# Attention scores on all 128 rows of the PE array: a full-height staging pair with placing DMAs, three weight buffers, keys' tiles ahead of queries' tiles

## The chip, the core and the metric

The kernel runs on one core of one Trainium2 chip. Inputs are in HBM; the working set lives in SBUF (128 partitions), matrix products go to eight PSUM banks of 128 x 512 fp32. The metric is the device time of one launch in microseconds (us), the median of the runs shown; one execution is taken with the hardware profiler and gives the rows below.

## What is computed

A decoder trunk of two layers on 512 tokens of width 1024. Each layer normalises x, projects it (one wide input projection), runs three token mixers in parallel, gates and merges them, and adds a gated per-layer embedding:

```python
h = rmsnorm(x, norm_g[i]);  proj = h @ w_in[i]
# A: 8 heads x 64, causal, with a cumulative log-forget bias
s = q @ k.T * 64**-0.5 + c[q] - c[k];  ya = softmax(s) @ v * silu(za)
# B: 8 query heads in 2 KV groups x 64: compressed, selected and sliding-window branches
yb = (g0*o_cmp + g1*o_sel + g2*o_win) * silu(zb)       # q and k rotated (rope)
# C: 4 heads, two 64-wide softmax maps each, 128-wide values
w = softmax(q1 @ k1.T) - lam * softmax(q2 @ k2.T);  yc = rmsnorm(w @ v) * silu(zc)
merged = sigmoid(mg_a)*(ya @ w_br_a) + sigmoid(mg_b)*(yb @ w_br_b) + sigmoid(mg_c)*(yc @ w_br_c)
x = x + merged @ w_out;  x = x + sigmoid(x @ w_ple_gate) * (p @ w_ple)
```

Every head's q and k are 64 wide. So a score product contracts over 64 rows, half of the PE array's 128.

## The kernel before

**Number format.** Each fp32 operand is split into a high part (rounded to the fp32r format) and a low part (the rest), and a product is three passes: hi x hi, lo x hi, hi x lo. `dense` does this for a weight tile: lines L731, L732, L733, each a matmul of 128 x 128 weights with 128 x 512 columns.

**Dense tiles.** A layer's weights come as 128-column tiles: `qa0` to `qa3` (queries of branch A, two heads each), `ka`, `va`, `za` (gate), then the same for B and C (`qb`, `ksb`, `kwb`, `vsb`, `vwb`, `zb`, `qc`, `kc`, `vc`, `zc`), the mixing gates `mga`/`mgb`/`mgc`, the branch projections `bra`/`brb`/`brc`, and `w1k`/`w1v`, four tiles each of a small hidden layer that compresses keys and values. A tile of `w_in` is 8 steps of three matmuls; `bra`, `brb`, `brc` have 4 steps; a `w1k` or `w1v` tile has 4 steps of two 256-column matmuls and is thus much shorter on PE than the others, though its weights are as large. SP loads a tile into one of RAW = 4 slots of `raw` (L589), ACT rounds it to `w_hi` in two halves (L1044), DVE subtracts to `w_lo` in two halves (L1278). `w_hi` and `w_lo` have two slots, so the conversion of tile t+2 starts when tile t is done. Results alternate between PSUM banks D0 and D1: tile t+2 may start only once ACT and DVE have emptied tile t's bank.

**Queries and keys.** For `qa` and `ka`, ACT copies the bank to a high part (L1111) and DVE makes the low part (L1425), straight into the places from which the scores read them. Rotated tiles (`qb`, `ksb`, `kwb`, `qc`, `kc`) are copied by ACT (L1120), SP swaps quarters of 32 partitions with four DMAs (L630), POOL multiplies by the sine (L683), DVE adds (L1519), ACT and DVE write high and low parts (L1151, L1521). A place holds two heads (or the two KV groups, or the two maps of C), one on partitions 0 to 63 and one on 64 to 127.

**Scores.** An attention unit is two heads; there are 12 units a layer, 0 to 3 of A, 4 to 7 of B, 8 to 11 of C. For a block i of 128 queries, an `S` step computes the scores of both heads against (i + 1) x 128 keys: three passes, in each one matmul on array rows 0 to 63 and one on rows 64 to 127 (L878), plus for A one more such pair that adds the forget bias (L884). The halves write to different banks, S0 and S1. A and C have one S step per block, B two (`sel`, `win`): 64 a layer, 128 in all. DVE masks and takes the maximum (L1530), ACT takes the exponential (L1158), PE transposes (L897, "T"), DVE or ACT copies (L539, L537), PE multiplies with the values (L919, "V").

**Order.** `make_schedule` writes one list of items, and every engine walks it. A stage s holds the attention steps of unit s and the dense tiles of `dense_tiles()[s]`; stage -1 comes ahead of all attention. Attention steps are spread among the dense steps; what follows a tile (swap, rot, ht, vcmp) comes a fixed number of dense steps after its end. Each engine is strictly in order, SP's queue too: a wait in front of one DMA holds up all DMAs behind it.

**After the attention** come a loop of `mgc` and `brc` tiles, `out`, and `gate`/`ple` tiles; ACT, DVE and PE walk the first two with hardware loops (`Fori`).

## Time and profile before

| | |
|---|---|
| median of 3 runs | 1543.6 us (1542.96 to 1544.0) |
| the profiled execution | 1546.29 us, of which the span from first to last instruction is 1544.5 us |
| mean granted clock of PE | 0.993 of full |
| PE busy (matmul) | 1500.4 us, 97% |
| PE weight loads, beside it | 1207.1 us, 78% |
| DVE / ACT / POOL busy | 942.2 (61%) / 636.7 (41%) / 75.3 us (5%) |
| all DMA queues | 129.49 MB, 31% of the 16 engines |
| dense matmuls, of the busy time | L731, L732, L733: 67% of the chain that ended last |
| score matmuls | L878: 768, L884: 64 |

A line of the profile is one group of instructions: line of the kernel, engine, operation, output<-inputs, shape, count. A matmul's shown duration includes the latency of the array, and matmuls overlap; what one costs is read from the distance between starts. A row of the timeline joins instructions of the same line that follow each other (xN). PEld is the weight load, which normally runs while the matmul ahead is still going. SPq is the queue of SP, which issues the DMAs.

### The profile page before, as it was taken

To read this page: it belongs to the slowest core of one execution; us is meant where nothing else is said; L and a number is where in the kernel's file an instruction comes from. 1 tells how busy PE (TensorE), PEld (TensorE's weight loads), DVE (VectorE), ACT (ScalarE), POOL (GpSimd) and SP (SyncE) were. 2 spreads that over 40 slices of the span, in tenths; PEclk is the share of its full clock that TensorE was granted. 3 is DMA by queue.
4 is the path that set the end of the run, shared out by engine and by line. 5 is a ranking of instruction groups with operands and counts; after the bars stand their busy time and mean duration, and the time that the engine had idled before them with its cause. 6 is when DMAs were issued, how large, how long until landed. Compare 5 with 4: busy or idle time off the path is not lost.

```text
span 1544.5 us, 22618 instructions
## 1 busy us (share of the span) xinstructions
PE 1500.4 (97%) x7957; PEld 1207.1 (78%) x7957; DVE 942.2 (61%) x2197; ACT 636.7 (41%) x1499; POOL 75.3 (5%) x80
## 2 busy tenths in 40 slices
PE   8999999999999999999999999999999999999997
PEld 6777777887787777888787787787887787788885
DVE  6866755555657776454576667655555676754544
ACT  6533434433344443343444334334333444334343
POOL 1000000000000010000100000000000000000011
PEclk9999999999999999999999999999999999999998
DMA  7223332222223332332342324222222233233321
GB/s 196 83 83 89 96 75 60 58 69 62 69 62 96 93 79 83 95 109 72 106 108 69 103 80 115 59 54 63 63 62 76 73 92 89 69 96 102 89 85 73
DMA packets 250300, 129.49 MB, mean 84 GB/s; under 512 B 45690, under 2 KB 245972, under 8 KB 250196
## 3 DMA queue, kind: packets, MB, share of 16 engines
q1 hardware_dynamic: 250196, 128.13, 31.1%
q8 instruction: 61, 1.00, 0.3%
q14 instruction: 43, 0.35, 0.1%
HBM read 118.67 MB, written 2.10 MB: 78 GB/s over the span
## 4 chain that ended last, share of the span: by engine, by line
PE 86%; DVE 6%; ACT 4%; issue 2%; DMA 1%; SPq 0%; POOL 0%; ACTq 0%; POOLq 0%; DVEq 0%
PE D L731 24%; PE D L733 22%; PE D L732 21%; PE Ob L919 7%; PE S L878 5%; PE T L897 4%; DVE w_lo L1278 2%; ACT w_hi L1044 1%; ACT probs L1158 1%; PE Mb L935 1%; PE Mb L845 1%; PE Ob L923 1%; PE Mb L812 1%; DVE probs L1530 0%; DVE y_lo L1612 0%
## 5 line engine op out<-in xcount | busy, mean ns | idle before, releaser
L731 PE MATMUL D<-h_hi,w_hi 128*128 128x512 f32 x1264 | 543.6, 430 | 12.5 <-DVE zs L1429 4.3
L733 PE MATMUL D<-h_lo,w_hi 128*128 128x512 f32 x1264 | 496.9, 393 | 0.0
L732 PE MATMUL D<-h_hi,w_lo 128*128 128x512 f32 x1264 | 495.2, 392 | 0.0
L1278 DVE TENSOR_TENSOR w_lo<-raw,w_hi 128x512 fp32r<-128x512 f32 (+2 forms) x504 | 295.2, 627 | 310.2 <-ACT w_hi L1044 310.1
L1044 ACT ACTIVATE w_hi<-raw 128x512 fp32r<-128x512 f32 (+2 forms) x504 | 264.7, 572 | 316.1 <-PE D L733 314.7
L731 PEld LDWEIGHTS D<-h_hi,w_hi 128*128 128x128 f32 x1264 | 239.2, 189 | 72.6 <-issue 20.8
L1158 ACT ACTIVATE probs<-probs,nmax 128x128 f32<-128x128 f32 (+3 forms) x256 | 141.9, 555 | 355.8 <-DVE nmax L1530 355.8
L733 PEld LDWEIGHTS D<-h_lo,w_hi 128*128 128x128 f32 x1264 | 237.9, 188 | 53.2
L732 PEld LDWEIGHTS D<-h_hi,w_lo 128*128 128x128 f32 x1264 | 240.1, 190 | 30.8 <-issue 0.5
L1530 DVE CUSTOM_DVE_ANT_0 probs<-S,maskb 128x128 f32<-128x128 f32 (+3 forms) x256 | 115.2, 487 | 49.2 <-PE S L878 30.3
L539 DVE COPY pT<-T 128x128 f32<-128x128 f32 (+3 forms) x160 | 77.6, 487 | 53.1 <-PE T L897 52.6
L919 PEld LDWEIGHTS Ob<-v_b,pT 128*128 128x128 f32 x640 | 90.5, 191 | 12.4 <-ACT pT L537 2.0
L897 PE MATMUL T<-ident,probs 128*128 128x128 f32 x560 | 98.0, 273 | 2.0 <-ACT probs L1158 2.0
L878 PE MATMUL S<-arena 64*128 64x384 f32 (+3 forms) x768 | 93.7, 349 | 0.9 <-DVE arena L1425 0.9
L731 PE MATMUL D<-y_hi,w_hi 128*128 128x512 f32 x224 | 93.9, 419 | 0.4 <-DVE y_lo L1612 0.4
L897 PEld LDWEIGHTS T<-ident,probs 128*128 128x128 f32 x560 | 72.3, 140 | 28.0 <-ACT probs L1158 5.6
L878 PEld LDWEIGHTS S<-arena 64*128 64x128 f32 x768 | 57.0, 185 | 45.5 <-issue 41.6
L733 PE MATMUL D<-y_lo,w_hi 128*128 128x512 f32 x224 | 87.9, 392 | 0.0
L732 PE MATMUL D<-y_hi,w_lo 128*128 128x512 f32 x224 | 87.5, 391 | 0.0
L919 PE MATMUL Ob<-v_b,pT 128*128 128x64 f32 x640 | 85.5, 264 | 0.3
L683 POOL TENSOR_TENSOR rb<-rs,sinT 128x512 f32<-128x512 f32 x28 | 36.4, 1300 | 970.0 <-DMA rs<-rx 596.0
L919 PEld LDWEIGHTS Ob<-v_ac,pT 128*128 128x128 f32 x480 | 67.7, 193 | 14.6 <-DVE pT L539 7.3
(243 smaller groups left out, 1499.3 us busy)
## 6 DMA issues: line engine op xcount, KB each, us to landing
raw<-in_w_in_dram SPq DMA_DIRECT2D x124, 512.0 KB, 3.9
raw<-in_w_in_dram SPq DMA_DIRECT2D x32, 256.0 KB, 3.7
raw<-in_w_out_dram SPq DMA_DIRECT2D x16, 512.0 KB, 4.0
raw<-in_w_ple_gate_dram SPq DMA_DIRECT2D x16, 512.0 KB, 4.1
rs<-rx SPq DMA_DIRECT2D x80, 64.0 KB, 2.0
raw<-in_cmp_w_k_dram SPq DMA_DIRECT2D x8, 512.0 KB, 3.8
raw<-in_cmp_w_v_dram SPq DMA_DIRECT2D x8, 512.0 KB, 3.8
raw<-in_w_br_a_dram SPq DMA_DIRECT2D x16, 256.0 KB, 2.9
```

Source lines behind the costliest of these rows:

```text
L539: eng.tensor_copy(pT[:, k % 2, 0:n], Tr[k % 2][:, 0:n]).then_inc(M["pt_dve_s"], 1)
L683: pool.tensor_tensor(rb[:], rs[:], sinT[:], ALU.mult).then_inc(M["pool_rot"], 1)
L731: pe.matmul(o, w_hi[:, sl, cs], hi[:, k, :], start=(k == 0), stop=False)
L732: pe.matmul(o, w_lo[:, sl, cs], hi[:, k, :], start=False, stop=False)
L733: ins = pe.matmul(o, w_hi[:, sl, cs], lo[:, k, :], start=False, stop=last)
L878: ins = pe.matmul(Sc[h][:, 0:n], qx[ps, qs], kx[ps, 0:n], start=(step == 0), stop=last)
L897: ins = pe.transpose(Tr[k % 2][:, j * P:(j + 1) * P], src[:, j * P:(j + 1) * P], ident[:])
L919: ins = pe.matmul(Ob[:, oc], pT[:, k % 2, j * P:(j + 1) * P], vs(j), start=(j == 0), stop=(j == i))
L1044: A(w_hi[:, sl, half], raw[:, ring(L, t, RAW), half], ACT.Copy).then_inc(M["act_hi"], 1)
L1158: A(probs[:, r % NP_, 0:n], probs[:, r % NP_, 0:n], ACT.Exp, scale=-1.0, bias=nmax[:, r % 8:r % 8 + 1], accum_out=sums[:, u % 2, i, c:c + ...
L1278: TT(w_lo[:, sl, half], raw[:, ring(L, t, RAW), half], f(w_hi[:, sl, half]), ALU.subtract).then_inc(M["dve_lo"], 1)
L1530: dve.tensor_tensor_reduce(probs[:, r % NP_, 0:n], Sc[r % 2][:, 0:n], maskb[:, S - n:S], -1.0, 3.0e38, ALU.add, ALU.min, nmax[:, r % 8:r % ...
```

## The change

1. **Scores on the whole array.** A query place now holds, for each head, high part and low part above each other on the 128 partitions; a key place holds for each head the high part twice and the low part twice. One matmul with the high keys then gives hi x hi and lo x hi at once, a second one with the low keys hi x lo and lo x lo. An S step becomes two matmuls per head on all 128 rows (L898, L899), with a third per head for A's bias (L902): four instead of six, or six instead of eight, and head 0 is complete before head 1 starts.
2. **Staging and placing.** ACT and DVE write the parts into one pair of buffers, `new_hi` and `new_lo`, and SP moves them to their places with four DMAs per tile (L659): of 64 x 512 for a query tile (512 KB in all), of 64 x 1024 for a key tile (1 MB in all). The S step that opens a unit waits for these DMAs (semaphore `put_s`); the next tile's write of `new_hi` waits for the placing of the one before.
3. **Room for it:** RAW is 3 instead of 4; `rb` is gone, the sine product is made in `rs` itself, so a swap now waits for DVE's use of the last one; `vbd` has its own buffer.
4. **Order of tiles:** in stage -1 `ka0` comes ahead of `qa0`; stages 1 to 3 are arranged anew; after `w1v3` the transposes `ht` and `vcmp` come 12 and 16 steps later instead of 6 and 8.
5. The hardware loops of ACT and DVE after the attention are written out (PE's stay), and a copy of the bias rows (L1473) is gone.

```diff
-RAW = 4
+RAW = 3
...
-    st = {-1: [("va", 0), ("va", 1), ("va", 2), ("va", 3), ("fg", 0), ("qa", 0), ("ka", 0), ("qa", 1)]}
+    st = {-1: [("va", 0), ("va", 1), ("va", 2), ("va", 3), ("fg", 0), ("ka", 0), ("qa", 0), ("qa", 1)]}
     st[0] = [("kcb", 0), ("ka", 1), ("za", 0), ("w1k", 0)]
-    st[1] = [("qa", 2), ("ka", 2), ("w1k", 1), ("ksb", 0), ("w1k", 2), ("za", 1)]
-    st[2] = [("qa", 3), ("w1k", 3), ("ka", 3), ("za", 2), ("vcb", 0)]
-    st[3] = [("qb", 0), ("w1v", 0), ("kwb", 0), ("w1v", 1), ("za", 3), ("w1v", 2), ("vsb", 0), ("w1v", 3), ("vwb", 0)]
+    st[1] = [("qa", 2), ("ka", 2), ("w1k", 1), ("za", 1), ("w1k", 2), ("qa", 3), ("w1k", 3)]
+    st[2] = [("vcb", 0), ("ka", 3), ("za", 2), ("w1v", 0), ("qb", 0), ("w1v", 1)]
+    st[3] = [("vsb", 0), ("w1v", 2), ("ksb", 0), ("w1v", 3), ("za", 3), ("kwb", 0), ("vwb", 0)]
...
-                follow.extend([[6, ("ht", t)], [8, ("vcmp", t)]])
+                follow.extend([[12, ("ht", t)], [16, ("vcmp", t)]])
...
+        q_st = [[part(6 * b + h) for h in range(2)] for b in range(2)]
+        k_at = [2, 8, 12]
+        KS, KW = 0, 2
+        new = sb("new", [P, 2 * S], F32R)
+        new_hi, new_lo = new[:, 0:S], new[:, S:2 * S]
...
+        def places(kind, n):
+
+            if kind[0] == "q":
+                q = q_st[n % 2]
+                return [(q[h][half((h + part_) % 2), :], new[half(h), part_ * S:(part_ + 1) * S])
+                        for h in range(2) for part_ in range(2)]
+            at = k_at[{"ka": n % 2, "ksb": KS, "kwb": KW, "kc": (n + 1) % 2}[kind]]
+            return [(part(at + 2 * h, 2)[half(g), :], new[half(h), :]) for h in range(2) for g in range(2)]
...
+                        if it[0] in ("end", "rot") and SPLIT_AT.get(tiles[it[1]][0]) == it[0]:
+
+                            kind, n, _ = tiles[it[1]]
+                            if it[0] == "end":
+                                sp.wait_ge(M["dve_evac"], dve_evac.after(it[1]))
+                            else:
+                                sp.wait_ge(M["qk_s"], rots.after(it[1]))
...
+                            for dst, src in places(kind, n):
+                                sp.dma_start(f(dst), f(src)).then_inc(M["put_s"], 16)
...
-                            for step, (qx, kx) in enumerate(((q_hi[b], ka), (q_lo[b], ka), (q_hi[b], kb))):
-                                last = step == 2 and m != "a"
-                                for h in range(2):
-                                    ps = slice(HD * h, HD * h + HD)
-                                    ins = pe.matmul(Sc[h][:, 0:n], qx[ps, qs], kx[ps, 0:n], start=(step == 0), stop=last)
...
+                            for h in range(2):
+                                if r >= 2:
+                                    pe.wait_ge(M["dve_max"], r - 1 + h)
+                                qx = q_st[b][h][:, i * P:n]
+                                k_hi, k_lo = keys(m, u, h)
+                                pe.matmul(Sc[h][:, 0:n], qx, k_hi[:, 0:n], start=True, stop=False)
+                                ins = pe.matmul(Sc[h][:, 0:n], qx, k_lo[:, 0:n], start=False, stop=m != "a")
...
                             if kind in ("qa", "ka"):
-                                if n >= 2:
-                                    act.wait_ge(M["pe_s"], rows_before[n - 1])
...
+                                if placed.after(t) > 1:
+                                    act.wait_ge(M["put_s"], 64 * (placed.after(t) - 1))
```

How the instructions move is best seen in three places. The first is on PE in stage 1, just after tile `ka2` (its last L733 is the third row). Names: D is the dense bank pair, Ob the output of V, arena holds the places of q and k and the input of w1k. Before:

```order
396 L731 MATMUL D<-h_hi,w_hi 128x512
397 L732 MATMUL D<-h_hi,w_lo 128x512
398 L733 MATMUL D<-h_lo,w_hi 128x512
399 L744 MATMUL D<-w_hi,arena 128x256 [waits dve_evac_0,dve_lo_0]
...
406 L745 MATMUL D<-w_lo,arena 128x256
407 L878 MATMUL S<-arena 128x384 [waits dve_max_0]
408 L878 MATMUL S<-arena 128x384 x5
409 L884 MATMUL S<-ck,selr 128x384 x2
410 L731 MATMUL D<-h_hi,w_hi 128x512 [waits dve_evac_0,dve_lo_0]
```

and now:

```order
413 L754 MATMUL D<-h_hi,w_hi 128x512
414 L755 MATMUL D<-h_hi,w_lo 128x512
415 L756 MATMUL D<-h_lo,w_hi 128x512
416 L938 MATMUL Ob<-v_ac,pT 128x64 [waits pt_dve_s_0]
417 L767 MATMUL D<-w_hi,arena 128x256 [waits dve_evac_0,dve_lo_0]
...
424 L768 MATMUL D<-w_lo,arena 128x256
425 L754 MATMUL D<-h_hi,w_hi 128x512 [waits dve_evac_0,dve_lo_0]
426 L755 MATMUL D<-h_hi,w_lo 128x512
427 L756 MATMUL D<-h_lo,w_hi 128x512
428 L898 MATMUL S<-arena 128x384 [waits dve_max_0]
```

The S step that stood between the short tile and the next full tile now stands after the first step of that tile; a V step stands in front instead.

The second place is the first S step of branch `win` in unit 4, on PE. Before, the six half-height matmuls waited for nothing but the score banks:

```order
863 L731 MATMUL D<-h_hi,w_hi 128x512
864 L732 MATMUL D<-h_hi,w_lo 128x512
865 L733 MATMUL D<-h_lo,w_hi 128x512
866 L878 MATMUL S<-arena 128x128 [waits dve_max_0]
867 L878 MATMUL S<-arena 128x128 x5
```

Now there are four, and the first waits for the placing of `kwb`:

```order
913 L754 MATMUL D<-h_hi,w_hi 128x512
914 L755 MATMUL D<-h_hi,w_lo 128x512
915 L756 MATMUL D<-h_lo,w_hi 128x512
916 L898 MATMUL S<-arena 128x128 [waits dve_max_0,put_s_0]
917 L899 MATMUL S<-arena 128x128
918 L898 MATMUL S<-arena 128x128 [waits dve_max_0]
919 L899 MATMUL S<-arena 128x128
```

`kwb` was the third tile of stage 3 and is now the last but one, so that its rotation falls into stage 4, three dense steps after the stage's begin.

The third place is SP's queue around the same tile, as it is now: the swap of `kwb`, two weight loads, then its placing (DVE's semaphore `qk_s` says that the rotated parts are ready), and behind it the swap of the next rotated tile:

```order
73 L643 DMA rs<-rx 32x512 [waits dve_rs_0,act_evac_0]
74 L643 DMA rs<-rx 32x512 x3
75 L602 DMA raw<-in_w_in_dram 128x8x128 [waits dve_lo_0]
76 L602 DMA raw<-in_w_br_a_dram 128x4x128 [waits dve_lo_0]
77 L659 DMA arena<-new 64x1024 [waits pe_dense_0,qk_s_0]
78 L659 DMA arena<-new 64x1024 x3
79 L643 DMA rs<-qf 32x512 [waits dve_rs_0,act_evac_0]
```

Before, SP had no DMA between rotation and scores.

## Rows read from the trace of the kernel before

**Rows 1.** The page: the costliest dense line: busy us, mean ns | idle before, releasers.

```profile
L731 PE MATMUL D<-h_hi,w_hi 128*128 128x512 f32 x1264 | 543.6, 430 | 12.5 <-DVE zs L1429 4.3 <-ACT rx L1120 2.7 <-DVE arena L1425 2.5
```

**Rows 2.** Timeline of PE (start us, duration us): an S step of B, 256 keys.

```profile
404.29 0.40 PE L733 MATMUL D<-h_lo,w_hi 128*128 128x512 f32 x1
404.61 0.62 PE L878 MATMUL S<-arena 64*128 64x256 f32 x6
...
405.50 0.40 PE L732 MATMUL D<-h_hi,w_lo 128*128 128x512 f32 x1
```

**Rows 3.** Timeline of PE: an S step of B, 512 keys.

```profile
380.86 0.39 PE L733 MATMUL D<-h_lo,w_hi 128*128 128x512 f32 x1
381.18 0.97 PE L878 MATMUL S<-arena 64*128 64x512 f32 x6
...
382.42 0.40 PE L732 MATMUL D<-h_hi,w_lo 128*128 128x512 f32 x1
```

**Rows 4.** Timeline of PE: an S step of A, 512 keys, with its bias.

```profile
199.09 0.39 PE L733 MATMUL D<-h_lo,w_hi 128*128 128x512 f32 x1
...
200.87 0.40 PE L732 MATMUL D<-h_hi,w_lo 128*128 128x512 f32 x1
```

**Rows 5.** Timeline of PE: full-height work between dense matmuls, and two 256-column ones.

```profile
215.84 0.39 PE L733 MATMUL D<-h_lo,w_hi 128*128 128x512 f32 x1
216.07 0.60 PE L897 MATMUL T<-ident,probs 128*128 128x128 f32 x4
...
216.74 0.40 PE L732 MATMUL D<-h_hi,w_lo 128*128 128x512 f32 x1
106.97 0.28 PE L744 MATMUL D<-w_hi,arena 128*128 128x256 f32 x1
107.09 0.28 PE L745 MATMUL D<-w_lo,arena 128*128 128x256 f32 x1
```

**Rows 6.** Timeline of PE, layer 0: waits behind short tiles, and matmuls after one.

```profile
106.26 0.40 PE L733 MATMUL D<-h_lo,w_hi 128*128 128x512 f32 x1
109.46 0.47 PE L731 MATMUL D<-h_hi,w_hi 128*128 128x512 f32 x1 [0.96 <-DVE arena L1425]
193.06 0.74 PE L731 MATMUL D<-h_hi,w_hi 128*128 128x512 f32 x1 [1.84 <-DVE zs L1429]
193.60 0.63 PE L732 MATMUL D<-h_hi,w_lo 128*128 128x512 f32 x1
214.41 1.08 PE L845 MATMUL Mb<-kcmpT,qf 128*128 128x64 f32 x8 [0.73 <-DVE vbd L1511]
```

**Rows 7.** Timeline of DVE, ACT and PE: the first S step of each layer.

```profile
58.43 0.57 ACT L1111 ACTIVATE arena<-D 128x512 fp32r<-128x512 f32 x1
62.00 0.68 DVE L1425 SCALAR_TENSOR_TENSOR arena<-D,arena 128x512 fp32r<-128x512 f32 x1
62.74 0.55 PE L878 MATMUL S<-arena 64*128 64x128 f32 x6 [0.87 <-DVE arena L1425]
818.90 0.69 DVE L1425 SCALAR_TENSOR_TENSOR arena<-D,arena 128x512 fp32r<-128x512 f32 x1
820.94 0.55 PE L878 MATMUL S<-arena 64*128 64x128 f32 x6
```

**Rows 8.** The swap's issues (one line's view), and a weight load (the page).

```profile
L630 SPq DMA_DIRECT2D rs<-rx x80: 512/591/600, 118.6 to 1307.2; - x80
DMA to landing us min/median/max: 1.9/2.0/3.5
raw<-in_w_in_dram SPq DMA_DIRECT2D x124, 512.0 KB, 3.9
```

**Rows 9.** Timeline of PE and DVE, layer 1: unit 4 opens.

```profile
970.15 0.55 PE L878 MATMUL S<-arena 64*128 64x128 f32 x6
974.22 0.69 DVE L539 COPY pT<-T 128x512 f32<-128x512 f32 x1
979.44 0.55 PE L878 MATMUL S<-arena 64*128 64x128 f32 x6
```

More of the change, by code:

```diff
@@ L314, in hybrid_trunk @@
             ysplit.add(it[1])
+    SPLIT_AT = {"qa": "end", "ka": "end", "qb": "rot", "ksb": "rot", "kwb": "rot", "qc": "rot", "kc": "rot"}
+    placed = Count()
+    for it in items:
+        if it[0] in ("end", "rot") and SPLIT_AT.get(tiles[it[1]][0]) == it[0]:
+            placed.add(it[1])
     DA0 = NM
@@ L449, in hybrid_trunk @@
         hid = y_f[:, 2, :].rearrange("p (a g b c) -> p a g b c", a=2, g=2, b=4)
+        vbd = sb("vbd", [P, 2, P])
         kcmpT = sb("kcmpT", [P, 2 * C32])
@@ L555, in landed_at, with keys @@
             return slot_sum[t % RAW] + 16 * ((t - T0) // RAW + 1)
-        def rot_dst(kind, n):
-            if kind == "ksb":
-                return ks_hi, ks_lo, None
-            if kind == "kwb":
-                return kw_hi, kw_lo, None
-            u = (4 if kind == "qb" else 8) + n
-            return (k_hi[u % 2], k_lo[u % 2], u) if kind == "kc" else (q_hi[u % 2], q_lo[u % 2], u)
+        def places(kind, n):
[5 more added lines that the diff above has]
+            return [(part(at + 2 * h, 2)[half(g), :], new[half(h), :]) for h in range(2) for g in range(2)]
+        def keys(kind, u, h):
+            at = k_at[{"a": u % 2, "sel": KS, "win": KW, "c": (u + 1) % 2}[kind]] + 2 * h
+            return part(at), part(at + 1)
         with nc.Block() as block:
@@ L618, in _ @@
                         sp.dma_start(dst, src).then_inc(M["par2_ld"], 16)
-                    for t in range(RAW, 6):
+                    for t in range(RAW, RAW + 2):
                         static_load(t)
@@ L627, in _ @@
                             if n > 1:
-                                sp.wait_ge(M["pool_rot"], n - 1)
+                                sp.wait_ge(M["dve_rs"], n - 1)
                             for a, b in ((0, 32), (32, 0), (64, 96), (96, 64)):
                                 sp.dma_start(rs[a:a + 32, :], src[b:b + 32, :]).then_inc(M["sw_ld"], 16)
-                        if it[0] == "end" and it[1] + 6 < T0 + 4:
-                            static_load(it[1] + 6)
+                        if it[0] == "end" and it[1] + RAW + 2 < T0 + RAW:
+                            static_load(it[1] + RAW + 2)
+                        if it[0] in ("end", "rot") and SPLIT_AT.get(tiles[it[1]][0]) == it[0]:
+                            kind, n, _ = tiles[it[1]]
[3 more added lines that the diff above has]
+                                sp.wait_ge(M["qk_s"], rots.after(it[1]))
+                            u = {"qa": n, "ka": n, "qb": 4 + n, "ksb": 4, "kwb": 4}.get(kind, 8 + n)
+                            if kind == "kwb":
+                                sp.wait_ge(M["pe_dense"], tile_of[("w1v", 3)] + 1)
+                            elif u >= 2:
+                                sp.wait_ge(M["pe_s"], rows_before[u - 1])
+                            for dst, src in places(kind, n):
+                                sp.dma_start(f(dst), f(src)).then_inc(M["put_s"], 16)
                     sp.wait_ge(M["dve_ysplit"], 12)
@@ L881, in _ @@
-                            if m == "a":
-                                for h in range(2):
-                                    ps, hh = slice(HD * h, HD * h + HD), 2 * u + h
-                                    pe.matmul(Sc[h][:, 0:n], selr[ps, hh:hh + 1].to_broadcast([HD, P]), ck[ps, 0:n],
-                                              start=False, stop=True).then_inc(M["pe_s"], 1)
+                                    need = [("qc", u - 8), ("kc", u - 8)]
+                                else:
+                                    need = [("qb", u - 4)] + [("ksb" if m == "sel" else "kwb", 0)] * (u == 4)
@@ new lines, in _ @@
+                                pe.wait_ge(M["put_s"], 64 * max(placed.after(tile_of[x_]) for x_ in need))
+                            n = (i + 1) * P
+                            for h in range(2):
[5 more added lines that the diff above has]
+                                ins = pe.matmul(Sc[h][:, 0:n], qx, k_lo[:, 0:n], start=False, stop=m != "a")
+                                if m == "a":
+                                    hh = 2 * u + h
+                                    ins = pe.matmul(Sc[h][:, 0:n], selr[:, hh:hh + 1].to_broadcast([P, P]), ck[:, 0:n],
+                                                    start=False, stop=True)
+                                ins.then_inc(M["pe_s"], 1)
@@ L1146, in _ @@
                             kind, n, s = tiles[t]
-                            hi_, lo_, u = rot_dst(kind, n)
                             act.wait_ge(M["dve_rs"], rots.after(t))
-                            if u is not None and u >= 2:
-                                act.wait_ge(M["pe_s"], rows_before[u - 1])
-                            A(hi_, rc[:], ACT.Copy).then_inc(M["act_rot"], 1)
+                            act.wait_ge(M["put_s"], 64 * (placed.after(t) - 1))
+                            A(new_hi, rc[:], ACT.Copy).then_inc(M["act_rot"], 1)
                         elif what == "S":
```

173 lines of the change are left out of this document (69 added, 104 removed).

## The prediction

> **What bounds the kernel now.** I began with the page. PE is busy 1500.4 of 1544.5 us, DVE 61%, ACT 41%, so the time changes with what PE has to do and with where it stands still. The costliest dense line [rows 1] is the sign of health to look for: its idle time over 1264 matmuls is 12.5 us, and the largest parts of that end with DVE `zs` (4.3), ACT `rx` (2.7) and DVE `arena` (2.5), all of them bank waits. Then I took the timeline of PE and read what one score step costs, as the distance between dense matmuls around it, since shown durations overlap. Last I read the waits of stages -1 to 4, where the tile order and the readiness of q and k change.
>
> **Term 1, the S steps: a gain.** What follows a dense matmul of 512 columns starts 0.23 us behind it (215.84 to 216.07) [rows 5] (0.227 over a whole tile of 24), so two dense starts with one between them would be 0.45 apart. A B step of 256 keys puts them 405.50 - 404.29 = 1.21 apart, so it costs 0.76 us [rows 2]; one of 512 keys 1.56 - 0.45 = 1.11 [rows 3]. The six matmuls stand for three simultaneous pairs: in A a fourth pair raises the 512-key step to 1.78 - 0.45 = 1.33 [rows 4], 0.22 more, which is one matmul's time and not two. Three pairs of 512 columns are thus 0.68, and 0.43 of the 1.11 is a fixed cost of the half-height excursion. It shows as a late start (0.32 instead of 0.23 after the last dense matmul) and in the weight loads that nothing hides. Full-height work has no such cost: four transposes between dense matmuls take 0.90 - 0.45 = 0.45 us, 0.11 each [rows 5]. The new step is four full-height matmuls. At 512 columns that is 4 x 0.227 = 0.91, at 256 it is 4 x 0.12 = 0.48 (the 256-column pair starts 0.12 apart) [rows 5], at 128 four times the 0.11 of a transpose. Gain: 0.20 at 512, 0.28 at 256, between these at 384 and 128; mean 0.235 over the 96 steps of B and C, 22.5 us. An A step becomes six matmuls: 1.36 against 1.33 at 512, 0.05 to 0.15 better at narrower widths, 2 us over 32 steps. Term 1: **-24.5 us**, bounds -18 (128-column fp32r matmuls cost half more than a transpose) to -27.
>
> The Trainium skill has a rule that speaks against the edit: TensorE: Matmul & The Clock Gate, Part 3, says that small-K matmuls on different row groups run at the same time and recommends packing them. The trace agrees for the pairs (0.22 for two). By that rule alone one slot of 0.16 on average is added to each B and C step and two to each A step, +25 us in place of the gain. But TensorEngine Tiling (Array Packing), Key Properties, says that a change of tiling mode drains TensorE; the fixed 0.43 us of rows 3 fits that.
>
> **Term 2, the order of tiles: a loss.** Where a short `w1` tile stands between two full ones, PE has about 1.3 us of work (last dense, eight matmuls 0.12 apart) and whatever else stands there, while the bank behind it is freed late: 3.20 us from the last dense start of `ka2` to the next full tile's first (106.26 to 109.46) [rows 6], of which the S step and the short tile filled all but 0.96. The same distance held at every stall for a q, k or gate tile (3.1 to 3.2, once 3.4 and once 4.0), 2.8 for a value tile. Before, these stalls are 0.59, 0.96, 0, 0.27, 0, 1.36, 1.84 or 1.28 and 0.41 for the eight short tiles of a layer, and 0.73 for `vbd` [rows 6], together 6.2 and 5.6 us. In the new order I fill in what stands behind each: `ka2`-`w1k1`-`za1` 1.7 (the S step has moved behind the first dense step, a V of 0.23 is left), `za1`-`w1k2`-`qa3` 0.6, `qa3`-`w1k3`-`vcb` 1.2, `za2`-`w1v0`-`qb0` 1.5, `qb0`-`w1v1`-`vsb` 0.7, `vsb`-`w1v2`-`ksb` 1.5, `ksb`-`w1v3`-`za3` 1.6, `za0`-`w1k0`-`qa2` 0.7, `vbd` 0 (16 steps later): 9.5 per layer. Term 2: **+7.5 us** for both layers, bounds +3 to +9.
>
> **Term 3, the first S step of a layer: a loss.** It waits for DVE's low part of the tile before last, ready at 62.68 in layer 0 and at 819.59 in layer 1; in the first PE stood 0.87 us, in the second not at all [rows 7]. Now four DMAs follow. The nearest row is the swap: four issues 0.63 us apart (0.59 each and a gap) and 2.0 to landing, 3.9 us [rows 8], with 64 KB each; the query tile's are 128 KB, a 512 KB load takes 3.9 to land where these take 2.0, so I take 4.3 (estimate), and for a key tile (4 x 256 KB) 5.4. Bounds are 3.9, the swap's own, and 9: at 1.9 us more for each 448 KB more, 1 MB one behind the other takes 2 + 4.3, and a weight load in front 2 more, rounded up. The dropped bias copy returns 0.4. But `new` is one pair: ACT may write `qa0` only when `ka0` is placed, at about 56.0 + 5.4 = 61.4 and not at 58.43 [rows 7], so DVE ends near 63.3 and the placing near 67.6; PE stands 5.8 instead of 0.87. In layer 1 the same gives 3.7 instead of 0. Term 3: **+8.6 us**, bounds +6 to +14.
>
> **Term 4, the first `win` step: a loss, twice.** `kwb` is rotated three dense steps into stage 4. PE reaches this step 9.3 us after the stage's first S [rows 9], 8.3 without the `vbd` stall and with shorter S steps. DVE has its copy of T done at 974.91 [rows 9], now about 0.6 earlier without the `vcmp` delay; then come add 0.69, ACT 0.6, subtraction 0.69, and 5.4 of placing: ready near 981.8, against PE at about 977.6. Behind this wait stands all of PE's stream. Term 4: 2 x 4.2 = **+8.4 us**, bounds +5 to +16.
>
> **Term 5, the clock.** After the stand of 1.84 us two dense starts are 0.54 apart (193.06, 193.60) [rows 6] and the next four 0.43, the lower level of 1.2 GHz: 1.2 us. After 1.36 nothing of the kind is seen. Four new stands of 4 to 6 us: **+3.5 us** net, bounds 0 to +6.
>
> **At no cost:** other places. The key tile nearest its use is ready 7.9 us ahead (DVE ends at 480.0, S at 488.0, and likewise for `kc2`, `kc3` and `ka1`), which covers 5.4; if that cover goes, rival B. RAW = 3: a load is issued with DVE's subtraction three tiles ahead, at least 7.5 us before its use against 3.9 to land [rows 8]. The swap's new wait is on a tile at least 12 steps older. SP meets its waits in DVE's own order, so no weight load is held up. Unrolled loops: PE has no idle in the stretches they cover. Two heads finishing apart let DVE begin 0.3 to 0.5 earlier: -1 at the three waits of T; +0.8 where stage 11 waits for DVE anyway.
>
> **Sum:** -24.5 + 7.5 + 8.6 + 8.4 + 3.5 - 0.2 = +3.3. The profiled execution took 1546.29 (span 1544.5), 2.7 above the median of 1543.6; the sum applied to the median gives **1547 us**.
>
> **Rivals.** *A, faster.* Placing takes 3.9 everywhere, the bank stalls are half absorbed since ACT and DVE catch up while PE stands, no clock drop: -24.5 + 4 + 6 + 5.5 - 0.5 = -9.5, 1534. For it: terms 2 to 4 come from chains that I lined up. Against: 3.20 us repeats too well.
> *B, much slower.* The key tile's megabyte moves at the rate of a chain of loads and takes 9 us. Then terms 3 and 4 grow by 3.6 four times, the slack of 7.9 at `kc1` to `kc3` and `ka1` is overrun by 1.1 in eight places, and the clock takes 2 more: +25 over my sum, 1572. It decides from 7.9 us of placing on. Against it: DMA queues are at 31%, and these rows are long.
> *C, the edit does not remove the fixed cost.* If the 0.43 belongs to S steps (their operands, two banks) and not to half-height work, 128 steps keep it: -24.5 turns to about +30, 1602. Against: it is absent at the transposes between the same dense matmuls [rows 5]. The packing rule above is this case's milder form.
>
> **Chances.** A measurement of this kernel tells 0.2% from no change, 3.1 us. My forecast 0.55: its own range 1541 to 1554 lies across that bound (slower 0.31, same 0.23, faster 0.01). A 0.28 (faster 0.26, same 0.02), B 0.12, C 0.05, both slower. Faster 0.27, same 0.25, slower 0.48. Range 1533 to 1561: down through A, up to where B begins.
>
> **What would show it.** L898 and L899 in place of L878, with dense starts around a 512-key B step 1.36 apart instead of 1.56; stalls of L754 near 1.5 us behind `w1k1`, `w1v0`, `w1v2`, `w1v3`; at the first S of each layer and at the first `win` step an idle of 4 to 6 us that ends with DMA `arena<-new`; that DMA's landing time. Wrong would be the forecast if those four idles are under 2 us (A), if every unit of C opens with one (B), or if the dense starts stay 1.8 apart (C).

## The result, and the profile after

| | before | after |
|---|---|---|
| median of the runs, us | 1543.8 (1542.96 to 1545.53, 4 runs) | **1572.94** (1570.07 to 1576.05, 4 runs) |
| ratio | | 1.0182 [1.017, 1.0195] |
| profiled execution / its span, us | 1546.29 / 1544.5 | 1573.54 / 1571.7 |
| PE busy, us | 1500.4 | 1495.3 |
| mean granted clock | 0.993 | 0.982 |

The kernel became 29 us slower. The forecast was 1547 (1533 to 1561): the direction was the likelier one named, the size was missed by 26 us, and the time lies outside the range. One execution among those of the experiments, of the kernel with the S steps alone, took 2958 us and is left out of its median. PE has 5 us less to do and still takes 27 us more of span, so the answer is in where it stands still and in its clock. The page after the change, beside [rows 1] and [rows 8] (the counterpart of the dense line, and S's line with a new releaser):

```profile
PE 1495.3 (95%) x7701; PEld 1248.0 (79%) x7701; DVE 932.4 (59%) x2195; ACT 632.2 (40%) x1499; POOL 74.8 (5%) x77
L754 PE MATMUL D<-h_hi,w_hi 128*128 128x512 f32 x1264 | 540.1, 427 | 17.6 <-DVE new L1434 6.9
L898 PE MATMUL S<-arena 128*128 128x128 f32 (+3 forms) x256 | 80.6, 323 | 24.2 <-DMA arena<-new 24.1
arena<-new SPq DMA_DIRECT2D x80, 256.0 KB, 4.7
arena<-new SPq DMA_DIRECT2D x96, 128.0 KB, 2.3
```

The waits of PE, the largest first (engine and line, what it waited for, us in total, times, longest):

```profile
PE S L898 <- DMA arena<-new: 24.1, 5, 7.8
PE D L754 <- DVE new L1434: 6.9, 4, 2.8
PE Ob L727 <- DMA y_q<-in_final_g_dram: 6.3, 1, 6.3
PE Mb L841 <- DVE y_f L1611: 5.2, 2, 2.6
```

Two of these were not there before: 24.1 us at `S` for the placing DMAs, and 5.2 at `Mb` (the step `ht`, the transposes behind the last `w1k` tile). The wait of 6.3 is the program's start and was 5.3 before. All waits of PE over 0.15 us add up to 65.7 us, and to 33.8 before.

The score step itself did what term 1 said. A B step of 512 keys, answering to [rows 3]: from the last dense start in front of it to the second one behind it are 393.91 - 392.52 = 1.39 us, where the same distance was 1.56 before. Less two dense distances (0.45) the step costs 0.94 here, and 0.91 as a median, against 1.11; nothing starts late in front of it or behind it.

```profile
392.52 0.39 PE L756 MATMUL D<-y_lo,w_hi 128*128 128x512 f32 x1
392.76 0.40 PE L898 MATMUL S<-arena 128*128 128x512 f32 x1
392.99 0.39 PE L899 MATMUL S<-arena 128*128 128x512 f32 x1
393.22 0.40 PE L898 MATMUL S<-arena 128*128 128x512 f32 x1
393.45 0.39 PE L899 MATMUL S<-arena 128*128 128x512 f32 x1
393.68 0.39 PE L754 MATMUL D<-y_hi,w_hi 128*128 128x512 f32 x1
393.91 0.39 PE L755 MATMUL D<-y_hi,w_lo 128*128 128x512 f32 x1
```

The first S step of layer 0, answering to [rows 7]: PE, ACT and SyncE in their timelines.

```profile
60.71 0.39 PE L756 MATMUL D<-h_lo,w_hi 128*128 128x512 f32 x1
68.87 0.45 PE L898 MATMUL S<-arena 128*128 128x128 f32 x1 [7.77 <-DMA arena<-new]
...
54.67 0.37 SPq L602 DMA_DIRECT2D raw<-in_w_in_dram  x1
55.27 3.40 SPq L659 DMA_DIRECT2D arena<-new  x4
64.63 2.38 SPq L659 DMA_DIRECT2D arena<-new  x4
63.22 0.60 ACT L1125 ACTIVATE new<-D 128x512 fp32r<-128x512 f32 x1 [5.46 <-DMA arena<-new]
```

The chain starts in the lower rows: the four DMAs of `ka0` are issued from 55.27 on, 0.6 us behind a weight load (54.67). ACT may write `qa0` into the staging pair only when they have landed, and resumes at 63.22, 8.0 us after the first issue. Then come ACT, DVE, `qa0`'s own four DMAs from 64.63, and S at 68.87, 4.2 later. PE stood 7.77 us. In layer 1 it stands 5.80. The first `win` step, layer 1, answering to [rows 9]:

```profile
1005.44 0.69 DVE L1525 TENSOR_TENSOR new<-rc,new 128x512 fp32r<-128x512 f32 x1 [0.70 <-ACT new L1163]
1006.16 3.08 SPq L659 DMA_DIRECT2D arena<-new  x4
1012.83 0.47 PE L898 MATMUL S<-arena 128*128 128x128 f32 x1 [5.15 <-DMA arena<-new]
```

The chain is the one of term 4, but the placing takes 6.7 us (1006.16 to 1012.83).

The wait at `Mb` has another cause:

```profile
153.36 0.60 PE L954 MATMUL Mb<-ident,y_q 128*128 128x128 f32 x4
157.28 0.47 PE L841 MATMUL Mb<-ident,tmp 64*128 64x64 f32 x2 [2.62 <-DVE y_f L1611]
152.61 3.00 DVE L1383 TENSOR_TENSOR v_b<-D,par 64x248 f32<-64x248 f32 x8
156.54 0.68 DVE L1611 SCALAR_TENSOR_TENSOR y_f<-Mb,zs 128x512 f32<-128x512 f32 x1
```

A Y step (L954) transposes a finished unit's output into the bank `Mb`, and DVE empties it (L1611). `ht` comes 12 dense steps behind `w1k3`, in both kernels. In the new order `w1k3` is the last tile of stage 1, so `ht` falls one dense step behind the Y step, and DVE has the eight instructions that empty `vcb0`'s bank (3.00 us) and a score step to do before it frees `Mb`. In the kernel before, 12 us lay between Y and `ht` (137.12 to 149.39) and nothing waited.

The clock is lower in the stretches in and behind these waits: it falls while PE stands (at 64.6, with S at 68.87) or up to 1.4 us after it goes on. One row per stretch (start to end, its length, busy us and number of instructions of PE, PEld, DVE, ACT and POOL, granted clock, DMA share, GB/s), the first one undisturbed for comparison:

```profile
300.00:312.00 12.00, 12.00 (x68) 10.14 (x67) 6.31 (x19) 4.93 (x15) 1.29 (x1) 1.00 0.26 67
64.60:74.80 10.20, 5.93 (x18) 4.89 (x19) 2.62 (x9) 3.01 (x7) 0.00 (x0) 0.50 0.63 154
242.10:248.90 6.80, 5.34 (x20) 4.66 (x20) 1.72 (x7) 1.87 (x7) 0.00 (x0) 0.50 0.06 17
842.80:849.60 6.80, 5.67 (x17) 4.72 (x18) 1.20 (x5) 2.76 (x6) 0.00 (x0) 0.50 0.68 171
1010.10:1016.90 6.80, 4.07 (x15) 3.64 (x16) 1.15 (x6) 1.20 (x5) 0.00 (x0) 0.50 0.26 69
156.70:163.60 6.90, 6.32 (x19) 5.13 (x20) 3.28 (x5) 1.97 (x5) 0.00 (x0) 0.51 0.01 2
```

Half clock is 1.2 GHz: dense matmuls start 0.427 us apart there and not 0.227. With three shorter stretches (119.2, 607.3, 1375.3) there are eight, together 48 us, against three with 10 us before (the one at the program's end left out in both). The two late ones, at 607.3 and 1375.3, stand behind waits of only 1.8 us; before, one of two such waits was followed by one. Adding up by how much the starts in them lie further apart than at the full clock, I get 19 us after and 5 before.

### The profile page after: what moved, and what is told of

Its sections match the earlier page's. It is cut to its first block, busy times and chain, and to the rows that moved or that the text cites. A ratio compares the mean times of both kernels' runs of the same rounds, so it can differ in the third digit from the quotient of the medians.

```text
span 1571.7 us, 21989 instructions
## 1 busy us (share of the span) xinstructions
PE 1495.3 (95%) x7701; PEld 1248.0 (79%) x7701; DVE 932.4 (59%) x2195; ACT 632.2 (40%) x1499; POOL 74.8 (5%) x77
## 4 chain that ended last, share of the span: by engine, by line
PE 79%; DVE 8%; ACT 4%; issue 3%; DMA 3%; SPq 1%; ACTq 0%; POOL 0%; DVEq 0%; POOLq 0%
PE D L754 21%; PE D L756 20%; PE D L755 20%; PE Ob L938 7%; PE T L916 4%; DMA arena<-new 3%; DVE w_lo L1288 3%; PE S L898 2%; PE S L899 2%; ACT w_hi L1059 2%; SPq L659 1%; ACT probs L1170 1%; PE Mb L954 1%; DVE v_b L1383 1%; PE Ob L942 0%
## 5 line engine op out<-in xcount | busy, mean ns | idle before, releaser
L1288 DVE TENSOR_TENSOR w_lo<-raw,w_hi 128x512 fp32r<-128x512 f32 (+2 forms) x504 | 289.5, 616 | 329.0 <-ACT w_hi L1059 328.8
L1059 ACT ACTIVATE w_hi<-raw 128x512 fp32r<-128x512 f32 (+2 forms) x504 | 259.1, 561 | 345.3 <-PE D L756 344.7
L898 PE MATMUL S<-arena 128*128 128x128 f32 (+3 forms) x256 | 80.6, 323 | 24.2 <-DMA arena<-new 24.1
L709 POOL TENSOR_TENSOR rs<-rs,sinT 128x512 f32<-128x512 f32 x28 | 36.7, 1309 | 1033.5 <-DMA rs<-qf 594.3
L899 PE MATMUL S<-arena 128*128 128x128 f32 (+3 forms) x256 | 81.7, 328 | 0.0
```

Of the source, the lines that this page charges most:

```text
L898: pe.matmul(Sc[h][:, 0:n], qx, k_hi[:, 0:n], start=True, stop=False)
L899: ins = pe.matmul(Sc[h][:, 0:n], qx, k_lo[:, 0:n], start=False, stop=m != "a")
L1059: A(w_hi[:, sl, half_], raw[:, ring(L, t, RAW), half_], ACT.Copy).then_inc(M["act_hi"], 1)
L1288: TT(w_lo[:, sl, half_], raw[:, ring(L, t, RAW), half_], f(w_hi[:, sl, half_]), ALU.subtract).then_inc(M["dve_lo"], 1)
```

## The experiments

All ratios are to the kernel before, run on the same chip beside them. "Us back" is the distance to the 1572.94 above; the kernel before stood at 1543.7 to 1544.1 beside most of them and at 1545.2 beside the last four on record (`kcb0`, the loads, and the two best versions), so there it can be 1.4 us more. The questions: is each of the waits its own cause (my reading), or do they share one, so that what is taken away in one place comes back in another? And how much of the time is standing still, how much the clock?

**The three parts of the change, one at a time.** The S steps alone, in the kernel before (full-height operands from the old places, nothing staged; each score then mixes two heads):

```
-for step, (qx, kx) in enumerate(((q_hi[b], ka), (q_lo[b], ka), (q_hi[b], kb))):
...
-        ins = pe.matmul(Sc[h][:, 0:n], qx[ps, qs], kx[ps, 0:n], ...)
...
+for h in range(2):
+    pe.matmul(Sc[h][:, 0:n], q_hi[b][:, qs], ka[:, 0:n], start=True, stop=False)
+    ins = pe.matmul(Sc[h][:, 0:n], q_hi[b][:, qs], kb[:, 0:n], start=False, stop=m != "a")
```

> The kernel before with its score steps alone made full-height (four matmuls, six in A, on 128 rows, reading the old places, so that scores mix two heads; nothing is staged or placed). Theory 1, the fixed cost of 0.43 us belongs to half-height work: 22 to 24 us faster than the kernel before, 1520 to 1523 us, with a 512-column B step at 0.91 instead of 1.11. Rival, the changed kernel lost its time in the score steps themselves (fixed cost stays, or 128-row fp32r products run slower): no gain or a loss, 1543 or more.

Measured: 1525.93 us, the median of three runs, ratio 0.9891 [0.9871, 0.9912]. That is 18 us by the medians, 20.4 by the spans of the profiled executions. Each step costs what term 1 forecast: medians of 0.45, 0.48, 0.72 and 0.91 us (128 to 512 keys) against 0.68, 0.76, 0.93 and 1.10, which over all steps, those of A included, comes to 23.9 us. The whole kernel gains less than that. It did not go into waits of PE: those over 0.15 us add up to 33.8 us in both kernels. Units 5 to 7 of layer 0, in which both kernels run at the full clock and PE is busy over 99% of the time, first before and then here:

```profile
271.90:447.20 175.30, 174.75 (x1032) 139.46 (x1031) 98.84 (x260) 69.02 (x186) 5.13 (x4) 1.00 0.25 63
267.50:438.30 170.80, 170.10 (x985) 144.55 (x984) 99.08 (x260) 69.11 (x187) 5.15 (x4) 1.00 0.25 65
```

The 24 S steps in them bring 4.5 us where the medians add up to 5.5. What takes the rest is not shown.

So the expectation's mechanism holds, its size was 2 us or more too large, and the rival (no gain) is out.

The tile order alone, in the kernel before (tiles written by their names):

```
-st[1] = [qa2, ka2, w1k1, ksb, w1k2, za1]
-st[2] = [qa3, w1k3, ka3, za2, vcb]
-st[3] = [qb0, w1v0, kwb, w1v1, za3, w1v2, vsb, w1v3, vwb]
+st[1] = [qa2, ka2, w1k1, za1, w1k2, qa3, w1k3]
+st[2] = [vcb, ka3, za2, w1v0, qb0, w1v1]
+st[3] = [vsb, w1v2, ksb, w1v3, za3, kwb, vwb]
```

(with `ka0` ahead of `qa0`, `ht` and `vcmp` 12 and 16 steps after `w1v3`, and the waits on operands that this order needs)

> The kernel before with the new order of tiles and the later ht and vcmp of w1v, half-height scores, no placing. Theory 1, the order alone costs bank waits and the wait of the transpose of w1k3 for bank Mb (2.6 us a layer): 9 us slower than before without any low clock, up to 15 with it, 1553 to 1558. Rival, the order costs nothing by itself and all waits come from placing: 1542 to 1546.

Measured: 1556.51, ratio 1.0072 [1.0049, 1.0096], 12.4 us over the kernel before, as expected. But it is not made of what the prediction thought: term 2 put 7.5 us on bank stalls, and the trace has this row, and its like with 2.42 us in layer 1, with nothing staged or placed anywhere:

```profile
147.43 0.47 PE L818 MATMUL Mb<-ident,tmp 64*128 64x64 f32 x2 [2.47 <-DVE y_f L1609]
```

The placing DMAs, cut to 8 of their columns (the places are set to zero at the start, and S reads mostly zeros):

```
-sp.dma_start(f(dst), f(src))
+sp.dma_start(f(dst[:, 0:8]), f(src[:, 0:8]))
```

> The changed kernel with all placing DMAs cut to 8 columns (same number, same waits; scores read places that are mostly zero). Theory 1, the megabyte of a key tile is what makes placing long (8.0 and 6.7 us instead of the swap's 3.9): the first S step waits about 3.5 and 2 us instead of 7.8 and 5.8, the first win step 2.3 instead of 5.1, and some stretches of low clock go: 1573 - 14 - 4 to 8, that is 1551 to 1555. Rival, the number of issues and the wait on a queue make the time, whatever the size: 1568 to 1573.

Measured: 1551.12, ratio 1.0047 [1.003, 1.0064], as expected: 21.8 us hang on the size of these transfers. Its waits say what is left when they are nearly empty (issue, landing, and the staging pair):

```profile
PE S L901 <- DMA arena<-new: 10.9, 4, 4.4
PE D L757 <- DVE new L1437: 5.7, 4, 1.6
PE Mb L844 <- DVE y_f L1614: 5.2, 2, 2.6
```

24.1 became 10.9. So 13 us of the 21.8 are time stood at S; the rest is mostly clock. One bank wait shrank too. Behind `w1k1` in layer 0 PE stood 1.63 us with the tile order alone and stands 1.63 here, but 2.84 in the changed kernel, because ACT's write of `ka2` waits for the placing of `qa2`:

```profile
117.61 0.60 ACT L1125 ACTIVATE new<-D 128x512 fp32r<-128x512 f32 x1 [1.22 <-DMA arena<-new]
119.15 0.74 PE L754 MATMUL D<-h_hi,w_hi 128*128 128x512 f32 x1 [2.84 <-DVE new L1434]
```

**The first `win` step.** The changed kernel with `kwb` one tile earlier:

```
-st[3] = [vsb, w1v2, ksb, w1v3, za3, kwb, vwb]
+st[3] = [vsb, w1v2, ksb, w1v3, kwb, za3, vwb]
```

> The changed kernel with kwb ahead of za3 in stage 3, so that its rotation and placing end inside stage 3. Theory 1, the wait of the first win step is a matter of one late tile: both idles of 5.1 us go, and with them two stretches of low clock, 1573 - 10 - 4 = 1557 to 1561. Rival, the time lost there is taken over by the next wait (a bank or Mb): 1568 to 1573.

Measured: 1554.6, ratio 1.0066 [1.005, 1.0083]: 18.3 us back for one tile's place, 2 more than expected. Both waits of 5.1 are gone, and unit 4 takes 55.2 us in both layers instead of 63.1 and 62.5, which is 15 of the 18. The rest goes with stretches of low clock that are there in one trace and not in the other.

**The first S step.** Three ways to shorten its wait. `ka0` ahead of the forget tile:

```
-st[-1] = [va0, va1, va2, va3, fg0, ka0, qa0, qa1]
+st[-1] = [va0, va1, va2, va3, ka0, fg0, qa0, qa1]
```

> The changed kernel with the first keys' tile ka0 ahead of the forget tile fg0 in each layer's opening, so that ka0's placing runs under fg0's matmuls and qa0's staging write no longer waits for it. Theory (the wait of 7.8 and 5.8 us of the first S step is ka0's placing followed by qa0's placing): the wait falls to about 1 to 2 us in each layer, some 10 us, and with it the low clock behind the wait, 3 us in each layer: 1557 us, between 1553 and 1563. Rival (the placing takes its 8 us wherever it starts, because of the weight load ahead of it, and qa0's placing is as late as before): 1568 us or more.

Measured: 1568.43, ratio 1.0155 [1.0142, 1.0168], 4.5 us back, and the expectation of 16 is refuted. PE still stands 5.1 and 3.7 us. `ka0` is placed in time now, but ACT comes to `qa0` late:

```profile
55.93 1.28 ACT L1157 ACT_TABLE_LOAD   x1
57.22 0.63 ACT L1157 ACTIVATE probs<-probs 8x512 f32<-8x512 f32 x1
57.76 1.14 ACT L1059 ACTIVATE w_hi<-raw 128x512 fp32r<-128x512 f32 x2
58.80 0.57 ACT L1125 ACTIVATE new<-D 128x512 fp32r<-128x512 f32 x1
```

ACT works off the forget tile's exponentials, with their table loads, and then the next weights, and writes `new` at 58.80; `qa0`'s DMAs are issued at 60.33, and their landing took 3.9 to 4.2 us each, where it was 2.2 to 2.3 at the same place in the changed kernel, behind a weight load issued 0.6 us ahead of them. The work between two tiles is not only cover for PE. It also stands in ACT's and DVE's queues ahead of the next tile.

> The changed kernel with the tile kcb0 moved from the first place of unit 0 to a place between ka0 and qa0, so that 5.5 us of dense matmuls lie between the two staging writes and the placing of ka0 (8 us) is done when qa0's tile ends. Theory (the first S step's wait is two placings in a row through one staging pair): TensorE's wait falls from 7.8 and 5.8 us to the tail of qa0's placing alone, 1 to 3 us in each layer, some 9 us, and the low clock behind it by 0 to 6: 1561 us, between 1556 and 1565. Rival (as putting fg0 between them showed, where only 4.5 us were gained: what stands between only moves the engines' other work onto qa0's staging write): 1566 us or more.

Its edit puts `kcb0` there instead:

```
-st[-1] = [va0, va1, va2, va3, fg0, ka0, qa0, qa1];  st[0] = [kcb0, ka1, za0, w1k0]
+st[-1] = [va0, va1, va2, va3, fg0, ka0, kcb0, qa0, qa1];  st[0] = [ka1, za0, w1k0]
```

Measured: 1569.53, ratio 1.0149 [1.0134, 1.0164], 3.4 us back (4.8 against the kernel before beside it): the rival's number again, and for the same kind of reason. DVE now empties `kcb0`'s bank in eight instructions (3.00 us), PE waits 2.84 us for that bank in layer 0 and 0.56 in layer 1, and S still waits 4.3 and 4.2:

```profile
62.61 3.00 DVE L1383 TENSOR_TENSOR v_b<-D,par 64x248 f32<-64x248 f32 x8
...
67.65 0.58 ACT L1125 ACTIVATE new<-D 128x512 fp32r<-128x512 f32 x1
...
69.92 2.48 SPq L659 DMA_DIRECT2D arena<-new  x4
```

The third way leaves the order alone and turns two DMAs round on SyncE:

```
-if it[0] == "end" and it[1] + RAW + 2 < T0 + RAW:
+early = it[0] == "end" and tiles[it[1]][:2] in (("qa", 0), ("ka", 0))
+if it[0] == "end" and not early and it[1] + RAW + 2 < T0 + RAW:
     static_load(it[1] + RAW + 2)
...
         sp.dma_start(f(dst), f(src)).then_inc(M["put_s"], 16)
+if early:
+    static_load(it[1] + RAW + 2)
```

> The changed kernel with the weight load that SyncE issues at the end of qa0 and ka0 put behind that tile's four placing DMAs instead of ahead of them. Theory (a key placing takes 6.7 us by itself and 7.3 to 8.9 with a 512 KB load issued 0.6 us ahead of it): ka0's placing lands in 6.7 us and S starts 1 to 1.5 us sooner in each layer, 1570 us, between 1567 and 1572; the loads themselves are not waited for. Rival (the placing takes its 8 us by itself, since 2048 packets have to go through): 1573 us and the same 8 us in the trace.

Measured: 1569.33, ratio 1.0164 [1.0149, 1.0179], 3.6 us back by the median and 2.8 by the ratios, whose intervals overlap (the changed kernel's begins at 1.017), so the time alone does not settle it. The mechanism is in the views of the placing line for `ka0`, first in the changed kernel, then in this one:

```profile
L659 SPq DMA_DIRECT2D arena<-new x4: 509/754/1255, 55.3 to 57.4; - x4
DMA to landing us min/median/max: 4.7/5.5/5.7
```

```profile
L660 SPq DMA_DIRECT2D arena<-new x4: 504/608/1286, 56.1 to 57.9; - x4
DMA to landing us min/median/max: 3.0/4.2/4.9
```

With the load behind it each piece lands about 1.2 us sooner, PE stands 6.7 and 4.8 instead of 7.8 and 5.8, and PE waits for no weight in these places. The expectation's rival speaks of 2048 packets; the trace has 256 of 4096 bytes for a key placing, and 1024 of 512 bytes for such a weight load.

**The step `ht`.**

```
-follow.extend([[12, ("ht", t)], [16, ("kcmp", t)]])
+follow.extend([[16, ("ht", t)], [20, ("kcmp", t)]])
```

> The changed kernel with the steps ht and kcmp of w1k's last tile at 16 and 20 instead of 12 and 16 steps after it, so that ht no longer stands right behind a Y step whose bank VectorE empties late. Theory (TensorE's wait of 2.6 us in each layer before ht is the scratch bank, and a low clock of 6.8 us follows it in layer 0): 5 us for the waits and 0 to 3 for the clock, 1566 us, between 1563 and 1569. Rival (the bank is late for whatever step takes it next, or qb0's and u=4's steps behind kcmp are late in its place): within 2 us of the changed kernel, 1571 or more.

Measured: 1566.56, ratio 1.0142 [1.0127, 1.0156], 6.4 us back, as expected. The wait on `Mb` is gone from the trace. A T step after it waits 1.2 us in each layer instead, so the standing still accounts for 3 us. The low clock of 6.8 us that stood behind the old wait in layer 0 is gone too, worth about 3 us by the spacing of its starts.

**How much is clock.** The waits stay, but PE runs matmuls of no use while it waits (`fill` is 30 and 22 at the first S step of the layers, 18 at the first `win` step):

```
...
+for _ in range(fill):
+    pe.matmul(Sc[0][:, 0:S], selr[:, 0:1].to_broadcast([P, P]), h_hi[:, 0, :], start=True, stop=True)
 pe.wait_ge(M["put_s"], ...)
```

> The changed kernel with matmuls of no use (128x512, 30 and 22 ahead of the first S step of the two layers, 18 ahead of the first win step of each) run into the S bank while TensorE would stand idle for the placing, before the same waits. Nothing else is changed, and no wait is taken away. Theory (the clock fell because TensorE stood idle, and dense matmuls 0.427 us apart instead of 0.227 behind these four waits cost about 3 us each): 1562 us, between 1558 and 1567. Rival (the low clock belongs to something else than the idle time, or is worth nothing): 1573 us, and up to 1577 where the added matmuls outlast the placing.

Measured: 1564.58, ratio 1.0124 [1.0109, 1.0138], 8.4 us back without any wait taken away. The stretch around the first S step, in the same columns as above:

```profile
60.00:76.00 16.00, 15.24 (x74) 12.33 (x73) 5.41 (x17) 5.13 (x12) 0.00 (x0) 1.00 0.65 165
```

Clock 1.00 where the changed kernel had 0.50 from 64.6 to 74.8. S starts at 69.20, 0.76 us after the last matmul of no use, and the first dense matmuls behind it are 0.23 apart. The first `win` steps of both layers are at 1.00 as well. The first S step of layer 1, where PE still stands 1.53 us, has a stretch of 3.4 us at half clock and not 6.8. So the low clock came with the standing still of these four places, and cost 2 us at each (8.4 by four). This does not tell what the clock costs at the other places.

**Together.** The kernel with three of the edits (`kwb`, `ka0` ahead of `fg0`, `ht`):

> The changed kernel with three edits together: kwb one place earlier (ahead of za3), ka0 ahead of fg0, and ht and kcmp four steps later. Theory (the three waits are independent, each with its own low clock behind it): 18 us (kwb alone, measured) + 16 (ka0) + 7 (ht) under the changed kernel, 1532 us, between 1528 and 1540, and so below both kernels. Rival (the gains overlap, since a wait that is taken away uncovers the next): 1544 us or more, no better than the kernel before.

Measured: 1544.6 over 11 runs, ratio 1.0008 [0.9998, 1.0018]: the time of the kernel before, 28 us back. The three alone had given 18.3, 4.5 and 6.4, together 29.2, so they do not overlap; 1532 was missed because `a_fg` had not given its 16.

Then the four edits, with `kcb0` between `ka0` and `qa0` instead of `fg0`, and the loads behind the placings:

> The changed kernel with kwb ahead of za3, ht and kcmp of w1k3 four steps later, kcb0 between ka0 and qa0, and the two loads behind the placings of qa0 and ka0. Theory (each wait has its own cause and goes alone): the run with three edits stood at 1544.6 us with 5.3 and 3.7 us of wait and a low clock of 6.8 us behind each first S step; 8 us of wait and 6 of clock go, 1531 us, between 1527 and 1537, and so 0.8% under the kernel before. Rival (unit 0 has a tile less beside its S and T steps now, and their waits take the place): 1540 us or more.

Measured: 1541.55 over 12 runs, ratio 0.9981 [0.9972, 0.9991]. It beats the kernel before by 0.2%, but not the 0.8% expected; the rival's 1540 is the number.

> As the run before it, and qa2 moved from the first place of unit 1 to the last of unit 0, which puts the dense work back that kcb0 took with it, and puts ka2's tile directly ahead of w1k1. Theory of unit 0's cover: where the run before it waits in unit 0, this one does not, and it stands 1 to 3 us lower. Rival (qa2's placing has to wait for unit 0's S steps, and SyncE's loads queue behind it): 2 us or more above the run before it.

```
-st[0] = [ka1, za0, w1k0];       st[1] = [qa2, ka2, w1k1, za1, w1k2, qa3, w1k3]
+st[0] = [ka1, za0, w1k0, qa2];  st[1] = [ka2, w1k1, za1, w1k2, qa3, w1k3]
```

Measured: 1540.0 over 8 runs, ratio 0.997 [0.9959, 0.998]: the fastest version that leaves nothing out, 0.3% under the kernel before and 2.1% under the changed one. Between it and the run before it lie 1.6 us, and the intervals of the two ratios overlap. Of its waits:

```profile
PE D L757 <- DVE zs L1440: 7.3, 7, 1.4
PE D L757 <- DVE new L1437: 4.0, 4, 1.4
PE S L901 <- DMA arena<-new: 3.9, 2, 2.7
PE D L757 <- DVE v_b L1386: 3.4, 2, 2.8
```

The placing costs 3.9 of its 24.1 us now. By the spans this version is 13.0 us above the one with the S steps alone. Waits make 9.9 of them: all bank waits at D add up to 22.5 us against 13.6, the waits at S to 3.9 against 0.9, and the rest to 2 less. PE's busy time makes the other 3.

## Why the prediction was wrong

In us of the profiled spans, after against before (+27.2 in all):

| step of the prediction | forecast | found |
|---|---|---|
| term 1, S steps | -24.5 | -23.9 by the steps' medians, -18.7 net |
| term 2, bank stalls behind short tiles | +7.5 | +3.3 |
| not in the prediction: `ht` waits for `Mb` | 0 | +5.2 |
| term 3, first S step of a layer | +8.6 | +12.7 |
| term 4, first `win` step | +8.4 | +10.3 |
| term 5, clock | +3.5 | +14 |
| all other waits | -0.2 | +0.4 |

The rows add up with the net value of term 1, which is what is left when the waits (+31.9) and the clock (+14) are taken off. The waits are from the traces; the clock is worked out from the starts in the slow stretches, as above.

Four steps failed, the largest first: the clock was sized at a quarter of what it cost (+3.5 against +14); the S steps' gain was summed from single steps and came to 18.7 and not 24.5; the placing that terms 3 and 4 rest on was taken as 5.4 us and took 6.6 to 8.9 (waits of 23 us against 17); and the wait of `ht` (5.2) was put at nothing without being looked at.

*Term 1 held at the step* (0.91 us against the 0.91 forecast at 512 keys), including the fixed 0.43 us of a half-height step that the kernel with the S steps alone does not have. Rival C is out, and with it the Trainium skill's packing rule (TensorE: Matmul & The Clock Gate, Part 3) as an argument against this change: here the six half-height matmuls cost more than the four full-height ones at 128, 256, 384 and 512 columns of B and C, and less only in A's 512-key step (1.33 against 1.39). But steps that were read between dense matmuls and multiplied by their number are not the kernel: some 5 us of the gain are missing both here and in the kernel with the S steps alone (20.4 us, of which 1.7 are a stretch of low clock fewer, so again 18.7). They are not in waits over 0.15 us; where they are is open.

*The missed step* is not in the prediction at all: `ht` behind `w1k3`. Term 2 asked of every tile that moved what stands ahead of it and behind it, for the banks D0 and D1 and for `vbd`, whose 0 held. It did not ask it of what follows a tile. `w1k3` moved to the end of stage 1, its `ht` came along 12 steps later, and there it met the Y step that uses the same bank `Mb`, which DVE frees late because `vcb0` is in its queue. The tile order alone has the wait with 4.9 us, and the `ht` edit takes it away.

*Terms 3 and 4* name the right places, the right chains and the right releasers, and one input was wrong: the key placing, 5.4 us in the text, took 6.6 to 6.8 with no load just ahead of it (twice 7.9) and 7.3 to 8.9 with a weight load issued 0.6 to 0.7 us ahead. The query's 4.3 was 4.1 to 4.2 alone (once 4.5), and 5.6 to 7.0 behind a load. The upper bound of 9 had both effects in it ("a weight load in front 2 more"); the value taken had neither. Since the staging pair makes `qa0` wait for `ka0`, the error enters term 3 whole. Term 4 has a slip as well: 970.15 + 8.3 is 978.45 and not 977.6, which would have made it 3.4 us a layer. In the trace PE is there 8.44 us after the stage's first S, DVE's write ends 6.9 after it (6.2 in the prediction) and the placing takes 6.6: 5.1.

*Term 5 is the largest miss.* It counted 1.2 us for each new stand, from one stand of 1.84 us before. With stands of 5 to 8 us the low clock lasted 6.8 to 10.2 us and not 3.4. That is 2 us at each of the four places by the matmuls of no use, 2.0 to 3.0 by the spacing of the starts. It also came with waits that had no part in the term: 2.6 and 2.8 us (156.7, 119.2) and 1.8 us (607.3, 1375.3), while the 2.6 us in layer 1 (929.38) had none behind them. The bound of +6 was set without a row of a long stand.

*Term 2* was sized too high: the distance of 3.20 us held less well than claimed, and the stalls after were 7.9 and 7.2 us per layer against the 9.5 forecast, of which 1.2 in layer 0 are the staging pair's and not the order's. By luck this error went against the others and hid part of them.

*Rival B's number (1572) was met by luck, its story half.* The key placing reached the 7.9 us from which it was to decide in five of twenty places, three of them behind a load; but the places `kc1` to `kc3` and `ka1` that it wanted overrun held, with at most 0.9 us of wait in any run, at `ka1`. So the 9 us that it put there did not come, and the clock and `ht`, which it did not have, brought about as much. *Nothing for unrolled loops* held too: the last three stages of each layer took the same time within 0.1 us in both kernels (66.2, 43.8 and 58.3 in layer 0), and with RAW = 3 no load was waited for beyond the first of the program.

The range failed because each term had a bound of its own, while the clock and the waits are one event: where a placing is late, the stand and the clock behind it grow together, and so can the next bank wait. The upper bounds of terms 3, 4 and 5 with the other two terms as forecast gave 1562, all five upper bounds 1570, and the range was cut at 1561. Even 1570 is short of the time, since the clock and `ht` had no row under them.

What stays open: why the pieces of a key placing (256 KB each) land 1.0 to 1.5 us apart where a whole 512 KB weight load lands in 3.9; and where the 5 us of term 1 went. Neither was tried.

## What to carry to other kernels

An edit that makes the bound engine's work cheaper and puts a transfer in front of it must be counted at the first use of what it moves (a layer's first S, a branch's first step), since later the slack hides it and at the opening nothing does; one tile's place in the order was worth 18 us here. Count a wait of a busy TensorE at its length plus what the clock takes behind it, which was 2 to 3 us at each stand of 5 to 8 us here, and give both one common error. When a tile moves, the steps that follow it at a fixed distance move too, and each has to be charged for what it lands behind. And what is moved in between as cover has to be read on all engines: twice here it covered TensorE and stood in ACT's or DVE's way to the very write that was to come sooner, and once, with `vcb0`, in the way of the bank that `ht` needed.
